# Two attention-like mixers on key tiles of 128, 128 and 16 rows, with products of 128 contraction rows, and six operand-making instructions moved in front of the memory's pieces

## The reference

```
# first block, each of its 2 layers: one wide projection feeds three mixers
# differential attention: 8 heads, two maps of width 64 per head, values of width 128
s1 = softmax(causal(q1 @ k1.T * 64**-0.5));  s2 = softmax(causal(q2 @ k2.T * 64**-0.5))
o  = rms_norm((s1 - lam * s2) @ v) * (1 - lam_init)          # per head, 272 x 272 weights
# retention: 4 heads, keys of width 128, values of width 256
w  = (q @ k.T) * decay(head)[i - j] * 128**-0.5 for j <= i, else 0
o  = rms_norm(w @ v)
# second block, even layer
h += even_mixer(h)     # latent attention (8 heads) beside a delta-rule recurrence (8 heads of 64)
h += memory_cross_attention(h, mem)   # its keys and values come from `mem` alone
```

## Time and profile before

| | |
|---|---|
| median of three runs | 2688.68 us |
| the profiled execution | 2694.21 us, its span 2692.4 us |
| TensorE matmul busy | 2571.2 us, 95% of the span |
| TensorE weight load busy | 2392.4 us, 89% |
| GpSimd busy | 1965.9 us, 73% |
| VectorE busy | 1435.6 us, 53% |
| ScalarE busy | 1346.2 us, 50% |
| mean granted TensorE clock | 0.980 of full speed |

### The profile page before, as it was taken

One profiled execution on the slowest core, in us unless ns is written; L12 is line 12 of the kernel. 1 busy time (PEld: TensorE's weight loads), 2 busy tenths in 40 slices (PEclk: granted clock), 3 DMA queues, 4 the chain that ended last, 5 costly groups with the idle time before them and its releaser, 6 DMA issues.

```text
span 2692.4 us, 49249 instructions
## 1 busy us (share of the span) xinstructions
PE 2571.2 (95%) x19268; PEld 2392.4 (89%) x19268; DVE 1435.6 (53%) x2602; ACT 1346.2 (50%) x2337; POOL 1965.9 (73%) x2182
## 2 busy tenths in 40 slices
PE   8999999999999999999999999978899998998999
PEld 8888889899999988889998998768789998788999
DVE  6875432357627875343457644554345436764550
ACT  5434444555645444446456655551265445564543
POOL 8856557799889856568898987340069998566997
PEclk9999999999999999999999999898999999999999
DMA  7423334455665433345457665120036665333665
GB/s 215 141 87 102 106 107 134 124 151 172 175 174 148 131 92 106 96 117 145 122 165 206 191 166 139 48 79 1 1 103 191 190 183 142 90 96 104 189 188 156
DMA packets 683221, 354.91 MB, mean 132 GB/s; under 512 B 11152, under 2 KB 681072, under 8 KB 682608
## 3 DMA queue, kind: packets, MB, share of 16 engines
q1 hardware_dynamic: 680464, 343.45, 44.2%
q10 hardware_dynamic: 2528, 8.31, 0.9%
HBM read 350.67 MB, written 1.05 MB: 131 GB/s over the span
## 4 chain that ended last, share of the span: by engine, by line
PE 70%; POOL 13%; DVE 9%; ACT 4%; issue 2%; DMA 2%; ACTq 0%; DVEq 0%
PE pb L276 69%; POOL wl L345 13%; ACT pool L299 1%; ACT wh L334 1%; DMA raw<-in_w_in 1%; DMA raw<-in_w_ffn_in 1%; DVE pool L1127 1%; PE pb L553 0%; DVE bx L3365 0%; DVE pool L1113 0%; PE pb L1358 0%; DVE pool L1141 0%; ACT pool L300 0%; DVE pool L1112 0%; DVE rsb L1809 0%
## 5 line engine op out<-in xcount | busy, mean ns | idle before, releaser
L345 POOL TENSOR_TENSOR wl<-raw,wh 128x256 fp32r<-128x256 f32 (+1 forms) x2164 | 1954.6, 937 | 716.3 <-ACT wh L334 715.4
L276 PE MATMUL pb<-xh,wh 128*128 128x272 f32 (+2 forms) x3104 | 944.4, 304 | 29.1 <-DVE pool L1845 9.5
L334 ACT ACTIVATE wh<-raw 128x1024 fp32r<-128x1024 f32 (+2 forms) x669 | 690.3, 1033 | 461.7 <-PE pb L276 280.2
L276 PE MATMUL pb<-xl,wh 128*128 128x272 f32 (+2 forms) x3104 | 893.3, 288 | 0.0
L276 PE MATMUL pb<-xh,wl 128*128 128x272 f32 (+2 forms) x3104 | 893.2, 288 | 0.0
L276 PEld LDWEIGHTS pb<-xh,wh 128*128 128x128 f32 x3104 | 595.2, 192 | 52.9 <-issue 21.8
L276 PEld LDWEIGHTS pb<-xl,wh 128*128 128x128 f32 x3104 | 595.5, 192 | 3.7
L276 PEld LDWEIGHTS pb<-xh,wl 128*128 128x128 f32 x3104 | 594.8, 192 | 0.0
L276 PE MATMUL pb<-pool 128*128 128x128 f32 (+15 forms) x2064 | 328.1, 307 | 32.3 <-DVE pool L1141 7.3
L276 PEld LDWEIGHTS pb<-pool 128*128 128x128 f32 (+7 forms) x2064 | 240.7, 177 | 95.2 <-issue 25.9
L276 PE MATMUL pb<-u2h,wh 128*128 128x256 f32 x840 | 239.8, 285 | 2.2 <-DVE u2l L647 2.2
(11 more groups left out here) (385 smaller groups left out, 3800.0 us busy)
## 6 DMA issues: line engine op xcount, KB each, us to landing
raw<-in_w_in SPq DMA_DIRECT2D x208, 512.0 KB, 3.6
raw<-in_ffn_w SPq DMA_DIRECT2D x120, 512.0 KB, 3.8
raw<-in_w_ffn_in SPq DMA_DIRECT2D x88, 512.0 KB, 3.8
raw<-in_w_branch SPq DMA_DIRECT2D x48, 512.0 KB, 3.9
raw<-in_od_w_in SPq DMA_DIRECT2D x41, 512.0 KB, 3.7
raw<-in_w_ffn_out SPq DMA_DIRECT2D x32, 512.0 KB, 4.0
raw<-in_ev_w_in SPq DMA_DIRECT2D x20, 512.0 KB, 3.9
raw<-in_w_out SPq DMA_DIRECT2D x16, 512.0 KB, 3.9
```

What stands on the lines that cost most here:

```text
L276: return e.matmul(out, lhsT=l, rhs=r, start=a, stop=z, skip_group_check=True)
L334: E.e.activation(hi, src, ACT.Copy).then_inc(*sig("weight_hi", ("hi", g)))
L345: E.e.tensor_tensor(lo[:, s, :], src[:, s, :], hi[:, s, :].bitcast(F32), SUB).then_inc(*sig("weight_lo", *[("lo", g, i) for i in ks]))
```

## The change

1. **Attention scores.** A new buffer `QZ` holds, for each of two heads in turn and for each map, the queries of 128 rows with the other map's 64 rows zero. A score product then contracts all 128 rows of `DK`. ScalarE fills `QZ` (`a_pad`, two copies of 64 x 272 for each head); VectorE clears the halves once in a layer.
2. **Key tiles.** `KT3` is 128, 128, 16. The turned weights take 272, 144 and 16 query columns; a tile of 16 queries is turned by a product with columns of the identity instead of `transpose`. The value products always contract 128 rows: the rows 16 to 127 of the last tile are zero in the weights and, in `DV`, cleared by GpSimd (128 x 1024, once in a layer, in `hgrn_prep`).
3. **Retention** uses the same tiles and offsets.
4. **Even mixer.** The operand making of `v_rw_main` becomes the background `rw_ops` of four steps between `rw_gaps` and `key_norm`; `LRS[0]` is cleared by GpSimd; the latent attention's buffers `MPB` and `MTW` move out of the way of `AR`, `BT` and `KT_`. The rate beside the memory's pieces goes from 0.75 to 0.8.

```diff
+KT3 = [(0, 128), (128, 128), (256, 16)]
+    QZ = pv(24064, [2, 2, NT])
 ...
+        e.memset(DV[:, 2, :], 0.0).then_inc(*sig("hg_zero", ("dv_pad", li)))      # g_hgrn_prep
+        yield
 ...
+    WT_OFF = (0, 288, 272)
+    WT = 432
 ...
         def blocks(self, qi):
             q0, nq, nk = self.qtiles[qi]
-            return [(ki, k0, kn, i * nq) for i, (ki, (k0, kn)) in enumerate(
-                (ki, t) for ki, t in enumerate(self.ktiles) if t[0] < nk)]
+            return [(ki, k0, min(kn, nk - k0), max(q0, k0), q0 + nq - max(q0, k0), ki * P)
+                    for ki, (k0, kn) in enumerate(self.ktiles) if k0 < nk]
 ...
     def pe_att
+        e.wait_ge(*at("at_zero", a.name))
 ...
+                if qi == 0:
+                    e.wait_ge(*at("at_pad", a.name, hh))
-                    t = mm(e, B[0:nq, 0:nk], a.q(hh, m_)[:, q0:q0 + nq], a.k(hh, m_)[:, 0:nk], True, not a.causal)
-                    if a.causal:
-                        t = mm(e, B[0:nq, nk - nq:nk], ident[0:nq, 0:nq], C("neg")[0:nq, 0:nq], False, True)
-                    t.then_inc(*sig("at_scores", ("at_scores", a.name, u, m_)))
+                    mm(e, B[0:nq, 0:nk], a.q(hh, m_)[:, q0:q0 + nq], a.k(hh)[:, 0:nk], True, False)
+                    mm(e, B[0:nq, nk - nq:nk], ident[:, 0:nq], C("neg")[:, 0:nq], False, True).then_inc(
+                        *sig("at_scores", ("at_scores", a.name, u, m_)))
 ...
-                for ki, k0, kn, off in a.blocks(qi):
-                    t = e.transpose(B[0:kn, off:off + nq], pb[0:nq, 0, k0:k0 + kn], ident[0:nq, 0:nq])
+                for ki, k0, kn, ql, qn, off in a.blocks(qi):
+                    if qn == P:
+                        t = e.transpose(B[0:kn, off:off + qn], pb[:, 0, k0:k0 + kn], ident)
+                    else:
+                        t = mm(e, B[0:kn, off:off + qn], pb[:, 0, k0:k0 + kn], ident[:, ql - q0:ql - q0 + qn], True, True)
 ...
-                        qs = min(q[0] for q in a.qtiles if q[2] > k0)
-                        v = a.v(hh, ki)
-                        t = mm(e, O[r0:r0 + v.shape[1], qs:a.nq_all], v, wt[ki][0:kn, qs:a.nq_all], ki == 0,
-                               ki == len(a.ktiles) - 1)
+                        t = mm(e, O[:, k0:NT], a.v(hh, ki), wt[ki][0:P, k0:NT], ki == 0, ki == len(a.ktiles) - 1)
 ...
+    def a_pad(E, a, hh):
+        if hh >= 2:
+            E.e.wait_ge(*at("at_scores", a.name, 3 * hh - 4, 1))
+        for m_, key in enumerate(((), (("at_pad", a.name, hh),))):
+            r = slice(64 * m_, 64 * m_ + 64)
+            E.e.activation(QZ[r, hh % 2, m_, :], DQ[r, hh, :], ACT.Copy).then_inc(*sig("at_exp", *key))
     def a_att                                     # a_pad(E, a, 0) first; then, behind a unit's exponentials:
+                if qi == 1 and hh + 1 < a.heads:
+                    a_pad(E, a, hh + 1)
 ...
     def v_diff(E, li):
-        E.e.wait_ge(*at("lam", li))
+        e, a = E.e, diff(li)
+        e.wait_ge(*at("lam", li))
+        for q in a.ready:
+            e.wait_ge(*at(*q))
+        W2 = RSb[:, 0:2 * WT].rearrange("p (a b) -> p a b", b=WT)
+        e.memset(QZ[64:P, :, 0, :], 0.0).then_inc(*sig("at_v"))
+        e.memset(QZ[0:64, :, 1, :], 0.0).then_inc(*sig("at_v"))
+        e.memset(W2[:, :, 0:NM], 0.0).then_inc(*sig("at_v"))
+        e.memset(W2[:, :, NT:NT + 2 * NM], 0.0).then_inc(*sig("at_v", ("at_zero", a.name)))
 ...
-                for ti, (t0, tn) in enumerate(TOK):                       # pe_ret and v_ret, three places
+                for ti, (t0, tn) in enumerate(KT3):
-                        m = mm(e, O[:, t0:NT], RV[0:tn, ti, c:c + P], RSb[0:tn, o:o + NT - t0], ti == 0, ti == 2)
+                        m = mm(e, O[:, t0:NT], RV[:, ti, c:c + P], RSb[:, o:o + NT - t0], ti == 0, ti == 2)
 ...
-    MPB, MTW = [pv(17664 + 384 * i, [384]) for i in range(2)], [pv(18688 + 384 * i, [384]) for i in range(2)]
+    MPB = [(pv(2048, [NS]), pv(2304, [P])), (pv(22912, [NS]), pv(2432, [P]))]
+    MTW = [pv(22528, [384]), rs[:, :, :].rearrange("p a b -> p (a b)")[:, 0:384]]
 ...
+    def v_rw_ops(E):                              # the body stood at the head of v_rw_main
         e.wait_ge(*at("rw_dec", 2))
-        e.wait_ge(*at("m_out", 7))
 ...                                               # AR in two steps, BT, then KT_ and DEC: four steps
     def v_rw_main(E):
-        e.memset(LRS[0], 0.0).then_inc(*sig("rw_v"))
+        e.wait_ge(*at("lr_zero", 0))
     def g_rw_main(E):
+        e.wait_ge(*at("rw_ar"))
+        e.wait_ge(*at("m_turn", 7))
+        e.memset(LRS[0], 0.0).then_inc(*sig("lr_zero", ("lr_zero", 0)))
         e.wait_ge(*at("mm", E.g - 1))
-        e.memset(LRS[1], 0.0).then_inc(*sig("lr_zero", ("lr_zero",)))
+        e.memset(LRS[1], 0.0).then_inc(*sig("lr_zero", ("lr_zero", 1)))
 ...
-        bg = mix(chain(E.bg("prep"), E.bg("mla")), chain(E.bg("rw_prep"), E.bg("rw_gaps"), E.bg("key_norm", 0, KS)), 1)
-        bg = memory_kv(E, 0, KS, VS, bg, 0.75)
+        bg = mix(chain(E.bg("prep"), E.bg("mla")), chain(E.bg("rw_prep"), E.bg("rw_gaps"), E.bg("rw_ops"), E.bg("key_norm", 0, KS)), 1)
+        bg = memory_kv(E, 0, KS, VS, bg, 0.8)
-        bg = memory_kv(E, 1, K1_, V1_, bg, 0.75, E.bg("key_norm", 1, K1_))
+        bg = memory_kv(E, 1, K1_, V1_, bg, 0.8, E.bg("key_norm", 1, K1_))
```

More of the change, by code:

```diff
@@ L1295, in __getitem__, with turned_weights, __init__ @@
             return self.base[r, c.start - self.q0:c.stop - self.q0]
[L1297 to L1305, removed]
-    class Att:
[L1310 to L1314, removed]
+    WT_OFF = (0, 288, 272)
+    WT = 432
+    def turned_weights():
+        return [[Off(RSb[:, WT * i + o:WT * i + o + NT - k0], k0) for o, (k0, kn) in zip(WT_OFF, KT3)] for i in range(2)]
+    class Att:
+        def __init__(self, name, heads, q, k, v, qtiles, ktiles, probs, turned, bk, st0, lam, ready, vready):
+            self.name, self.heads, self.q, self.k, self.v = name, heads, q, k, v
+            self.qtiles, self.ktiles, self.probs, self.turned = qtiles, ktiles, probs, turned
+            self.bk, self.st0, self.lam, self.ready, self.vready = bk, st0, lam, ready, vready
             self.units = [(hh, qi) for hh in range(heads) for qi in range(len(qtiles))]
-            self.nq_all = sum(q_[1] for q_ in qtiles)
         def score_banks(self, u):
-            return self.bk[0:2] if self.maps == 2 else (self.bk[u % 2],)
+            return self.bk[0:2]
         def stats(self, u):
@@ L1363, in pe_att @@
                     wt = a.turned[hh % 2]
-                    O, r0 = banks[a.bk[3 + hh % 2]], a.row(hh)
+                    O = banks[a.bk[3 + hh % 2]]
                     for uu in range(u - len(a.qtiles), u):
@@ L1428, in v_att @@
                         e.wait_ge(*at("at_o", a.name, hh - 2))
-                    for ki, k0, kn, off in a.blocks(qi):
-                        t = e.tensor_copy(wt[ki][0:kn, q0:q0 + nq], banks[a.bk[2]][0:kn, off:off + nq])
+                    for ki, k0, kn, ql, qn, off in a.blocks(qi):
+                        t = e.tensor_copy(wt[ki][0:kn, ql:ql + qn], banks[a.bk[2]][0:kn, off:off + qn])
                     t.then_inc(*sig("at_wt_v", ("at_turned", a.name, u - 1)))
@@ L1495, in diff @@
[L1495 to L1501 removed]
+                    e.wait_ge(*at("at_o", a.name, hh))
@@ L3078, in v_rw_gaps, with other_rw_ops @@
         yield
+    def v_rw_ops(E):
+        e = E.e
+        e.wait_ge(*at("rw_dec", 2))
+        for c in range(2):
+            cs = slice(c * P, (c + 1) * P)
+            e.scalar_tensor_tensor(out=AR[:, :, c, 0, :], in0=KK[:, :, cs], scalar=-1.0, in1=EA[:, :, cs], op0=MLT, op1=MLT)
+            m = e.tensor_tensor(AR[:, :, c, 1, :], R_[:, :, cs], EP[:, :, cs], MLT)
+            if c == 0:
+                yield
+        m.then_inc(*sig("rw_v"))
+        yield
+        e.wait_ge(*last("rw_v"))
+        e.tensor_tensor(BT, AA, EM, MLT).then_inc(*sig("rw_v", ("rw_bt",)))
+        yield
+        e.wait_ge(*at("rw_bt"))
+        e.tensor_tensor(KT_, RK1, EM, MLT)
+        e.tensor_tensor(DEC.unsqueeze(2), CW[:, :, P + 63:P + 64], CW[:, :, 63:64], SUB).then_inc(*sig("rw_v", ("rw_ar",)))
+        yield
+    def other_rw_ops(E):
+        for _ in range(4):
+            yield
     def pe_rw_gaps(E):
@@ L3724, in walk @@
             w_in("dk", "rope", bg, 0.8, dst=DK, rope=("p2", "c2", "s2", 1.0))
-            w_in("dv", "tm", bg, 0.8, dst=DV, toks=TOK, tiles=8)
+            w_in("dv", "tm", bg, 0.8, dst=DV, toks=KT3, tiles=8, free=[("dv_pad", li)])
             w_in("rq", "rope", bg, 0.8, dst=RQ, rope=("p1", "c1", "s1", 1.0))
```

162 lines of the change are left out of this document (65 added, 97 removed).

## The result

The changed kernel takes 2669.64 us (median of 4 runs, 2667.66 to 2673.06) against 2690.07 us (4 runs) for the kernel before: ratio 0.9926, 95% interval 0.9906 to 0.9946. That is 20 us less, where 52 were forecast, and 2.6 us above the upper end of the stated range (2667). The profiled execution took 2673.06 us with a span of 2671.2, 21.2 us under the profiled execution of before (2694.21).

A forecast was written before the change was run, and what follows sets the result against it. TensorE was taken to bound the kernel, its matmul rows busy 95% of the span. Savings of 52.5 us, costs of 2.0, 2.0, 1.0 and 1.5, and -6.0 for the mixer gave -52.0: 2637 us, range 2622 to 2667.

The forecast's parts named there:

- Fill of `DV` on GpSimd: HGRN preparation: 1024 columns, 0.9 us, twice, queued before a piece's split; +1.0 us, bounds 0 and 1.8.
- scores, 32 units: Attention: 32 units each lose four changes between 64 and 128 contraction rows, 0.81 us a unit; -25.9 us.
- 16-query scores: Attention: 16 units of 16 queries save two row changes, 0.4 us each; -6.4 us.
- turned tiles: Attention: the 16-key part becomes a product instead of a turning, 0.05 us more, 32 times; +1.6 us.
- values: Attention: a head's value products fall from 1.50 to 0.91 us, 16 heads; -9.4 us.
- start of attention: Start of each layer's attention: VectorE's clearing delays the first scores by 1.0 us; +2.0 us for two layers.
- denser background: TensorE's waits for turned copies grow as the stretch shrinks by 14%; +2.0 us, bounds 0 and 8.
- memory's pieces: Rate 0.8 puts one or two more steps in front of `mem_x`; +1.5 us, bounds 0 and 2.5.
- `rw_main`: Even mixer's start: operands already exist, so TensorE's standstill for `DEC` goes; -6.0 us, floor 4.6, ceiling 6.6.
- Rival 2: The gap is not the change of rows; fresh float32 operands may each pay it, only columns go; 2682 us, chance 0.11.
- Rival 1: With less TensorE time another engine takes over and half the gain is given back; 2663 us, chance 0.18.
- Rival 3: Attention: ScalarE's pads come late and set each head's start, making the kernel slower; 2709 us, chance 0.05.

The follow-up runs named there:

- experiment 1: Changed kernel with the fill of DV's last tile made by VectorE at the start of hgrn, not by GpSimd in hgrn_prep: 2647.65 us.
- experiment 2: Kernel before with only the DV fill added on GpSimd at the end of hgrn_prep: 2706.81 us, ratio 1.0065.
- experiment 5: Changed kernel with GpSimd's DV fill moved from the end of hgrn_prep to eight steps into the HGRN mixer's background: 2654.73 us.
- experiment 10: Changed kernel with GpSimd's DV fill moved within hgrn_prep, ahead of the six fills of AT0 to AT2: 2656.66 us.
- experiment 6: Changed kernel with DV filled by VectorE and differential attention's score products reading 64 rows again, padded copies still made: 2676.94 us.
- experiment 3: Changed kernel with the 16-query part turned by a transpose of all 128 query rows, only needed columns copied: 2653.06 us.
- experiment 4: Changed kernel with the rate beside the memory's pieces back at 0.75 from 0.8: 2667.57 us.
- experiment 8: Changed kernel with DV filled by VectorE and the even mixer's operands and LRS[0] fill back at the start of v_rw_main: 2660.57 us.
- experiment 9: Experiment 7's kernel with the six fills of AT0 to AT2 also moved from GpSimd to VectorE: 2637.89 us.
- experiment 11: Changed kernel with DV filled by VectorE and whole transposes for the 16-query block, rate left at 0.8: 2641.70 us.
- experiment 7: Changed kernel with three edits: DV filled by VectorE, whole transposes for the 16-query block, memory's pieces at rate 0.75: 2636.57 us.

## Why the prediction was wrong

**The step that failed** is "Fill of `DV` on GpSimd ... +1.0", bounds 0 and 1.8. Its row was right: the fill takes 0.95 us. The price was wrong, about 22 us, since I asked only what queues behind the fill on GpSimd (a split, with buffers to spare) and not what GpSimd's work does to VectorE beside it: the fill moves GpSimd's run so that a VectorE instruction stands over 13 us, and TensorE waits behind that one's queue. Experiments 1 and 2 show from both sides that the fill is the cause, experiments 5 and 10 that its place matters. Why one place is unlucky stays open. This step is 21 of the 31 us between the forecast and the profiled execution; with the fill on VectorE the kernel takes 2647.65 us, inside the forecast's own range of 2624 to 2651. That it lies there is in part luck, since the other terms missed in both directions. The trace of before had the warning, the `tensor_scalar` of 10.16 us beside the fills and splits, which I had not read: the median of that line is 0.69 us, its longest 10.16.

The other terms, us over both layers:

| term | forecast | measured | from |
|---|---|---|---|
| scores, 32 units | -25.9 | -24.8 | 1.72 to 0.94 with 144 keys, 2.14 to 1.37 with 272; experiment 6 |
| 16-query scores | -6.4 | -4.3 | 0.76 to 0.49 each |
| turned tiles | +1.6 | +7.9 | 0.23 more for 32, 0.03 more for 16; experiment 3 |
| values | -9.4 | -7.0 | mean of 1.71 to mean of 1.28, waits included |
| start of attention | +2.0 | +3.6 | TensorE's waits of 1.4 and 2.2 for VectorE's clearing |
| denser background | +2.0 | +0.1 | waits for turned copies, 4.0 before and 4.1 after (in the values' row already) |
| retention | -12.4 | -12.9 | pieces 96 to 120 and 296 to 320 |
| fill of `DV` | +1.0 | +21.9 | preparation, both layers |
| memory's pieces | +1.5 | +6.8 | in this pair of profiles; some 4 by experiment 4 |
| `rw_main` | -6.0 | -6.9 | pieces 446 to 450; experiment 8: 5.4 |

The first five rows make -24.6, where both attentions measured -25.2 by their pieces. With that -25.2 and the last four rows the sum is -16.3; small shifts elsewhere, none over 2 us in a stretch, make it -21.2.

- *The change of rows* was read rightly, 0.20 us each, and experiment 6 prices it on its own. Rival 2 is refuted: a changed unit with fresh operands in both maps takes 0.94 us where its columns alone are 0.91, so no load shows. The rule of the Trainium skill ("TensorE: Matmul & The Clock Gate", Part 3) that was weighed there does not describe this stretch; the same part also lets a load run ahead when it targets the background weight buffer, and no run here shows which buffer a load uses.
- *Turned tiles* lay outside their bounds. I bounded two short loads and two short matmuls by their 16 columns. The timeline has the second row start 0.31 us after the first: the plain float32 product costs 0.23 us more than no product, where a further transposed block costs 0.1. Nothing in the trace before was so short with 128 rows beside transposes, and I should have taken the wider bound of the values' 16-column product, 0.25 us, there too.
- *The start of attention* was priced for VectorE by GpSimd's clearing rate, 1.0 us a layer with 1.5 as the bound. TensorE's first scores wait 1.4 us for the last clearing (L1522) in layer 0 and 2.2 in layer 1. The *denser background*, which was to cost 2.0, cost next to nothing.
- *`rw_main`* came out 6.9 us shorter, 0.3 above what I had called the ceiling. Experiment 8 gives 5.4 for the move; in its profile 1.6 us of the stretch's gain stays without it.
- *The rate of 0.8* was bounded by 2.5 us and cost 6.8 in this pair of profiles, some 4 by all. With it TensorE waits 3.0 us for `bx` there (ScalarE's L300, three times) and 2.5 for a turned copy of latent attention (L2638); with 0.75 the first is 0.9 and the second no longer among the waits of 0.7 us or more. The moved operands are not the cause (experiment 8).
- *Rival 1* came true in size only. Half the gain was given back, but not by an engine that became the bound: GpSimd's busy time rose by 2.6 us in all.
- *Rival 3*: no wait for the pads appears among TensorE's waits; layer 0's attention keeps TensorE busy 138.5 of 141 us.

## What to carry to other kernels

Before putting even a microsecond of work on GpSimd, look through VectorE's lines for an instruction whose longest time is many times its median; if GpSimd is running without a pause beside it, the new work can cost what VectorE's queue costs, not its own length. Since such a hold comes and goes with the place of the work and from one execution to the next, compare several runs and price a change by stretches. Make all of a stretch's matmuls contract over the same number of rows: where the trace shows long products back to back, the step between them, less columns, is the price of a change (0.20 us here). Line two traces up by a repeated instruction before explaining their totals: gains of 50 us and losses of 29 lay under a difference of 21.

## What the runs showed of the hardware

- A VectorE instruction on SBUF can be held while GpSimd makes some 20 instructions back to back: 13.54 us in place of a median of 1.26. Most are not: in experiment 9 two started in the middle of such a run and took 0.73 and 0.70 us, and of the 814 to 854 VectorE instructions in a profile that read no PSUM and start while GpSimd is busy, 2 to 7 are held. Held ones occur in every profile here, 64 in all; what they take beyond their medians is from 13 us in sum (experiment 9) to 47 and 48 (the changed kernel and experiment 4), 29 in the kernel before. In all 64 GpSimd worked without a pause for the whole time by which the instruction was too long. In none of the 13 profiles did a VectorE instruction that reads PSUM take over 1.6 us.
- The Trainium skill ("SBUF — State Buffer", Who interferes with whom) has the two engines share one pair of ports under an exclusive lock, for VectorE instructions with two SBUF inputs or in a two-port mode, held "for the whole instruction". The kinds held here fit, and so does PSUM. By that rule alone a wait would end with GpSimd's instruction, after 0.7 to 1.3 us; here a hold spans 3 to 21 of them. What lets the held one in was not found; in the hold at 85.88 us it comes in at 98.8, where GpSimd's instruction takes 1.19 us in place of 0.71.
- These holds may be a good part of why runs of one kernel differ: among the profiled executions of four near kernels, 13 us held goes with 2638.7 us (experiment 9), 17 with 2635.2 (3), 26 with 2644.3 (11) and 43 with 2652.8 (7). That is a correlation over four kernels that are not the same, and not a test.
- A float32 product of 16 columns beside transposes cost 0.23 us, twice what a whole 128-column transpose cost (0.11).
- TensorE stood 9.96 us for a held VectorE instruction and was granted 0.50 of its clock for the first 3 us behind that, 0.72 for the next 4.
